# Gate and up projections of a two-layer encoder as seven block products, with the down projection as a phase of its own

## What is computed

```
mixed = jnp.concatenate([y_dil, y_na, y_conv], axis=-1) @ w_out
x = x + rmsnorm(mixed, g_post_mix)
hf = rmsnorm(x, g_pre_ffn)
f = (jax.nn.silu(hf @ w_gate) * (hf @ w_up)) @ w_down
return x + rmsnorm(f, g_post_ffn)
```

## Time and profile before

| | |
|---|---|
| time, median of 3 runs | 3253.07 us (3248.07 to 3254.09) |
| span of the profiled execution | 3252.3 us |
| busy: PE | 3189.5 us (98%) |
| busy: DVE, ACT, POOL | 46%, 29%, 28% |
| chain that ended last: PE, DVE, the engines' own issue | 88%, 7%, 2% |

### The profile page before, as it was taken

One profiled execution on the slowest core, in us unless ns is written; L12 is line 12 of the kernel. 1 busy time (PEld: TensorE's weight loads), 2 busy tenths in 40 slices (PEclk: granted clock), 3 DMA queues, 4 the chain that ended last, 5 costly groups with the idle time before them and its releaser, 6 DMA issues.

```text
span 3252.3 us, 42998 instructions
## 1 busy us (share of the span) xinstructions
PE 3189.5 (98%) x17580; PEld 2721.1 (84%) x17580; DVE 1507.1 (46%) x3072; ACT 937.1 (29%) x1816; POOL 903.9 (28%) x643
## 2 busy tenths in 40 slices
PE   9999999999999999999999999999999999999998
PEld 7888887888888888888878888878888888888887
DVE  6766657163333332333687666562533333333336
ACT  5433444441111111111344334444411111111112
POOL 1211113553222222221332121135622222222223
PEclk9999999999999999999999999999999999999999
DMA  3111002231111111110321110121311111110113
GB/s 146 45 54 51 23 34 81 79 130 52 39 40 39 34 38 39 40 39 33 128 83 49 51 48 29 42 82 70 124 54 38 39 39 39 39 39 33 39 40 123
DMA packets 50484, 184.29 MB, mean 57 GB/s; under 512 B 8049, under 2 KB 11761, under 8 KB 46833
## 3 DMA queue, kind: packets, MB, share of 16 engines
q1 hardware_dynamic: 47984, 173.68, 15.4%
q10 hardware_dynamic: 2304, 7.87, 0.6%
HBM read 144.81 MB, written 28.84 MB: 53 GB/s over the span
## 4 chain that ended last, share of the span: by engine, by line
PE 88%; DVE 7%; issue 2%; ACT 1%; DMA 1%; SPq 0%; POOL 0%; POOLq 0%; DVEq 0%; ACTq 0%
PE PS L1807 26%; PE PS L1809 26%; PE PS L1808 26%; PE PS L1959 3%; PE PS L1928 3%; PE PS L1943 2%; DVE PT L1557 1%; DVE XL L1390 1%; PE PS L1844 1%; DVE YO L1386 1%; DVE YO L1383 1%; DMA EYE<-small 0%; PE PS L1903 0%; ACT PT L1088 0%; DMA X<-mixed 0%
## 5 line engine op out<-in xcount | busy, mean ns | idle before, releaser
L1807 PE MATMUL PS<-XH,WH 128*128 128x512 f32 (+1 forms) x3648 | 1324.5, 363 | 19.8 <-DVE XL L1390 6.1
L1809 PE MATMUL PS<-XH,WL 128*128 128x512 f32 (+1 forms) x3648 | 1298.0, 356 | 0.0
L1808 PE MATMUL PS<-XL,WH 128*128 128x512 f32 (+1 forms) x3648 | 1297.1, 356 | 0.0
L1807 PEld LDWEIGHTS PS<-XH,WH 128*128 128x128 f32 x3648 | 691.3, 190 | 144.6 <-issue 25.2
L1809 PEld LDWEIGHTS PS<-XH,WL 128*128 128x128 f32 x3648 | 691.3, 190 | 100.9
L1808 PEld LDWEIGHTS PS<-XL,WH 128*128 128x128 f32 x3648 | 692.1, 190 | 92.2
L812 POOL TENSOR_TENSOR WL<-RAW,WH 128x1024 fp32r<-128x1024 f32 x188 | 448.7, 2406 | 361.1 <-ACT WH L984 361.1
L835 POOL TENSOR_TENSOR SG<-SG,RS 128x512 f32<-128x512 f32 x132 | 147.6, 1118 | 992.9 <-ACT SG L1127 992.9
L1627 DVE TENSOR_TENSOR ACC<-ACC,PS 128x512 f32<-128x512 f32 (+1 forms) x480 | 286.2, 598 | 245.3 <-PE PS L1809 244.0
L1807 PE MATMUL PS<-HH,WH 128*128 128x512 f32 (+1 forms) x1056 | 377.2, 357 | 3.6 <-DVE ACC L1627 2.0
L1809 PE MATMUL PS<-HH,WL 128*128 128x512 f32 (+1 forms) x1056 | 376.8, 357 | 0.0
(11 more groups left out here) (128 smaller groups left out, 3017.8 us busy)
## 6 DMA issues: line engine op xcount, KB each, us to landing
RAW<-w_in SPq DMA_DIRECT2D x48, 512.0 KB, 3.6
RAW<-w_gate SPq DMA_DIRECT2D x44, 512.0 KB, 3.4
RAW<-w_up SPq DMA_DIRECT2D x44, 512.0 KB, 3.5
RAW<-w_down SPq DMA_DIRECT2D x44, 512.0 KB, 3.7
X<-parked SPq DMA_DIRECT2D x6, 2048.0 KB, 7.3
RAW<-w_out SPq DMA_DIRECT2D x16, 512.0 KB, 4.0
parked<-YO SPq DMA_DIRECT2D x4, 2048.0 KB, 6.6
mixed<-YB ACTq DMA_DIRECT2D x8, 640.0 KB, 2.9
```

The source lines that it names most:

```text
L1807: nc.tensor.matmul(out, wh, xh, start=first, stop=False)
L1808: nc.tensor.matmul(out, wh, xl, start=False, stop=False)
L1809: return nc.tensor.matmul(out, wl, xh, start=False, stop=last)
```

## The change

Gate and up are written as one 2 x 2 block product. The model dimension is cut in two halves (4 tiles each) and so are the tokens of a group; gate and up of one unit are the two block rows of the weights; the seven products of the Strassen-Winograd scheme take the place of the eight block products. Their weight blocks are `A11`, `A12`, `A22` as loaded and four sums `S1` to `S4`; their token operands are `B11`, `B21`, `B22` and four sums `T1` to `T4`. Each product is 4 tiles x 3 matmuls into one PSUM bank.

- The tokens fall into group 0 (tokens 0 to 767, halves of 384) and group 1 (768 to 1279, halves of 256). A turn is one unit and one group: seven products, 84 matmuls, in three banks a, b, c. There are 44 turns in 27 visits: five visits of group 0 alone, 17 of both, five of group 1 alone. A visit loads its weights (1 MB), and DVE, ACT and POOL make the sums and the high and low parts of all seven blocks one visit ahead.
- The norm is applied to the tokens before the product (`normed`), so the two multiplications by `RS` behind it fall away. The recombination (`partial`: u2, u3, gate2, gate1, up2, hid1) is on DVE, with the copy of the first product on ACT (`first_copy`) and the second half's multiplication on POOL (`hidden2`).
- The hidden units go to memory (`store_hidden`) and come back (`load_hidden`) for the down product, now a phase after all gate and up turns: nine stages of two units and a last one of four, over six PSUM banks.
- The output projection and the norms around it go by four chunks (384, 384, 256, 256). In the passage to layer 1 the projections start only after the last down group, and POOL in place of DVE makes the low parts of chunks 0 and 1.

The core of the diff:

```
+OCHUNKS = ((0, 384), (384, 384), (768, 256), (1024, 256))
-STAGES = FT // 2
-END = STAGES - 1
+AHEAD = 5
+VISITS = [(u, (0,)) for u in range(AHEAD)] + [(u, (0, 1)) for u in range(AHEAD, FT)] + \
+         [(u, (1,)) for u in range(AHEAD)]
+TURNS = [(v, u, g) for v, (u, gs) in enumerate(VISITS) for g in gs]
+PRODUCTS = ("A11", "S2", "A12", "S3", "S1", "A22", "S4")
+OPERAND = {"A11": "B11", "A12": "B21", "A22": "T4", "S4": "B22", "S1": "T1", "S3": "T3", "S2": "T2"}
+END = 9
...
+            def turn_products(L, t):
...
+                for name in PRODUCTS:
+                    m, where = BLOCK[name], {"A11": "a", "A12": "a", "S1": "c", "S4": "c"}.get(name, "b")
...
+                    if name == "A12":
+                        pe.wait_ge(s_first, TURN[L, t])
+                    elif name == "S3":
+                        pe.wait_ge(s_u2, TURN[L, t])
+                    elif name == "A22":
+                        pe.wait_ge(s_u3, TURN[L, t])
+                    elif name == "S4":
+                        pe.wait_ge(s_gate2, TURN[L, t])
...
+                    for kk in range(4):
+                        last = products(PS[:, bank(t, where), 0:n], GH[v % 2][:, m, kk, :], GL[v % 2][:, m, kk, :],
+                                        CH[g][of][:, kk, :], CL[g][of][:, kk, :],
+                                        where not in opened and kk == 0, kk == 3, True)
```

What POOL runs, turn by turn (`TURNS`), in the changed kernel (`low` are low parts: `combination_low` of a token operand, 128 x 1024 in group 1, `raw_low` and `weight_sum_low` of a weight block, 128 x 512):

```
+                for t, (v, _, g) in enumerate(TURNS):
+                    first = t == 0 or TURNS[t - 1][0] != v
+                    if t in (2, 3):
+                        for k in range(KT):
+                            add(e, "x", t, k)
+                    if t == 5:
+                        for name in POOL_LOW[1]:
+                            combination_low(L, 1, name)
+                    if first and v + 1 < NV:
+                        raw_low(L, v + 1, 0)
+                        raw_low(L, v + 1, 1)
+                        if t in (2, 3):
+                            invert(e, "x", t)
+                        if t == 5:
+                            hidden2(L, t)
+                        weight_sum_low(L, v + 1, "S3")
+                        raw_low(L, v + 1, 2)
+                        weight_sum_low(L, v + 1, "S4")
+                    if t != 5:
+                        hidden2(L, t)
```

More of the change, by code:

```diff
@@ L526, in build @@
         s_yo = sem("yo")
-        s_gate = sem("gate")
-        s_sig = sem("sig")
-        s_sgr = sem("sgr")
-        s_h = sem("h")
+        s_pair = [sem(f"pair{i}") for i in range(2)]
+        s_wsum = sem("wsum")
+        s_whi = sem("whi")
+        s_wlo_raw = sem("wlo_raw")
+        s_wlo_v = sem("wlo_v")
+        s_wlo_p = sem("wlo_p")
+        s_xn = sem("xn")
+        s_mixsum = sem("mixsum")
+        s_chi = sem("chi")
+        s_clo_v = sem("clo_v")
+        s_clo_p = sem("clo_p")
+        s_product = sem("product")
+        s_first = sem("first")
+        s_u2 = sem("u2")
+        s_u3 = sem("u3")
+        s_gate2 = sem("gate2")
+        s_gate1 = sem("gate1")
+        s_silu2 = sem("silu2")
+        s_silu1 = sem("silu1")
+        s_up2 = sem("up2")
+        s_hid1 = sem("hid1")
+        s_hid2 = sem("hid2")
+        s_hout = [sem(f"hout{i}") for i in range(2)]
+        s_hin = [[sem(f"hin{i}{t}") for t in range(2)] for i in range(3)]
         s_hh = sem("hh")
@@ L666, in taps, with load_hidden @@
+            def load_hidden(L, part, t):
+                f = PARTS[part][2][t]
+                for turn in turns_of(f):
+                    sp.wait_ge(s_hout[turn % 2], stored(L, turn))
+                sp.dma_start(HF[HOME[part]][t][:, :], hidden[f, :, :]).then_inc(s_hin[HOME[part]][t], 16)
             def taps(L, j):
@@ L773, in _ @@
[L773 to L780 removed]
+                residual_mixed(e, 0)
+                store_mixed(e, 0)
+                residual_mixed(e, 1)
+                load_pair(L, 0)
+                store_mixed(e, 1)
@@ L781, in _ @@
+                for part in range(1, len(PARTS)):
+                    load_weights(L, part)
+                    load_hidden(L, part, 0)
+                    load_hidden(L, part, 1)
+                    if part == END and L + 1 < DEPTH:
+                        for unit in "kqv":
+                            load((L + 1, unit, 0))
                 e = 2 * L + 1
-                residual(e, 0)
-                residual(e, 1)
+                for c in range(NCH):
+                    residual(e, c)
@@ L953, in _ @@
+                for part in range(1, len(PARTS)):
+                    for f in PARTS[part][2]:
+                        low((L, "d", f))
+                e = 2 * L + 1
+                more_layers = L + 1 < DEPTH
+                for part in "kqv" if more_layers else ():
+                    low((L + 1, part, 0))
                 for k in range(KT):
@@ L974, in _ @@
                 else:
-                    scaled_gate(L, f + 1, 2)
+                    for k in range(KT):
+                        add(e, "y", 1, k)
+                    invert(e, "y", 1)
                     invert(e, "y", 2)
@@ L1743, in _ @@
+                for s in range(END):
                     for c in range(NCH):
@@ L1836, in sum_squares @@
                     pe.wait_ge(s_sq, SQUARE[e, kind, c, KT - 1])
-                    squares += [SQ[kind][:, m, :] for m in range(2)]
+                    squares += [pair_of(e, kind, c)[:, m, :] for m in range(2)]
                 else:
```

1370 lines of the change are left out of this document (777 added, 593 removed).

## The result

The changed kernel takes 3221.78 us (median of 4 runs, 3214.52 to 3224.54) against 3251.04 us for the kernel before beside it: a ratio of 0.9907, 95% interval 0.9893 to 0.9921. The gain is 29 us where 45 were forecast.

What follows compares the result with a forecast made beforehand. PE, busy 98% of the span, was taken as the bound; matmuls -119.6, output projection +5, waits +70, passage -3 and end +2.5 sum to -45 from 3252.3, forecasting 3208 us, range 3158 to 3243.

Steps and rivals of the forecast that it cites:

- main case: Whole kernel: the forecast sum with stalls of 45 to 95 us, giving 3183 to 3233 us; chance 0.60.
- matmul term: Gate and up: 1848 matmuls of each width replace 609.4 us per layer by 549.6, -119.6 us for both layers.
- Rival D: Gate and up: narrower matmuls cost more than the line says, 55 us for both layers, 3263 us; no separate chance.
- the clock: Gate and up: waits of several us lower PE's clock, costing 2.5 us more per layer.
- the hand-over from the output projection: Start of gate and up: PE waits for operands and their low parts, 5.5 us per layer (3 to 10).
- turns 1 to 6: Early gate and up: DVE and POOL need 97.8 us against PE's 77.9, so PE waits 20 us per layer.
- the visits of group 1 alone: Late gate and up: 11.3 us of work against 10.3, plus two down-weight low parts: 6 us per layer (0 to 12).
- Rival A: Gate and up: waits mostly absorbed, 12 us per layer, giving -91 us and 3162; chance 0.24 for 3145 to 3183.
- Rival B: Mixed visits: blocked DVE operations make each of 68 turns lose 1.3 us, 88 us in all, 3296; no separate chance.
- Rival C: Turns 1 to 6: waits chain up with low clock, 50 to 55 us per layer, 3235 to 3247; chance 0.07.
- The end: Last down stage and tail of the kernel: 53.3 us in place of 50.8, +2.5 us (0 to +7).
- The passage: Passage to layer 1: 24 us of waits and low clock in place of 26.9, -3 us (-8 to +8).

Runs made afterwards that it cites:

- no_lows: Changed kernel without POOL's five low parts of turn 5, PE taking the high part twice in group 1 instead: 3202.88 us.
- lows_dve: Changed kernel with the five low parts of group 1's operands made by DVE in place of POOL: 3209.47 us.
- late_steps: Changed kernel with DVE's steps 5 to 7 of chunks 2 and 3 put behind the next turn's u2: 3214.17 us.
- best: Changed kernel, eight visits of group 0 alone, group 1's low parts on DVE, operand work and norm steps spread over turns, end reordered: 3180.16 us, ratio 0.9785.
- double_early: Changed kernel with POOL making each weight low part twice in visits 7 to 21, the hidden product ahead of three low parts: 3219.88 us.

## Why the prediction was right, and where it was off

**The forecast's direction and mechanism held.** 3221.8 lies in 3158 to 3243 and in the main case's 3183 to 3233. Work of DVE and POOL that excludes each other makes PE wait on turns 0 to 6. For turns 5 and 6 no_lows and lows_dve show it. For turns 2 and 3 it is argued, from late_steps (the wait moved from u2 to u3) and from best (the same steps over more turns, and less waiting); no run takes POOL's work away there. That the total came within 14 us is in part luck: the matmuls gave 16 us more than forecast, and the rest cost 29 us more.

**The matmul term was too small by 16 us.** "96 of 256 take the rest" was the step that failed in it. The 192 wide matmuls of a stage do not all cost 0.2273: a down stage of 27.98 us less 48 narrow ones at 0.120 leaves 0.2315 for each of its 96 wide ones, and the fourth unit's 48 in the next gate and up stage take 11.15 us (1150.68 to 1161.83), 0.2323 each. I had given that rest to the narrow ones. These cost 0.1184 in the turns (9.94 / 84). The midpoint taken for 384, 0.1749, measures 0.1748 (14.68 / 84), so nearly the whole error is 1848 x 0.0041 = 7.6 us per layer. Rival D is refuted with it.

**Beside the matmuls the phases cost 95 us, not 70, and the term that was mis-sized is the clock.** PE's idle time was forecast at 32.5 us per layer and measures 28.5. By places: the hand-over from the output projection 5.5 and 3.7, turns 1 to 6 20 and 20.4, the visits of group 1 alone 6 and 2.7, the hand-over to the down phase 1 and 1.7 (for the low part of the last hidden value). The hand-over came out shorter although group 0's operands are 128 x 1536 and not the 1024 that my sum used (the low part for which PE waited 3.1 us took 3.4 us on POOL, DVE's next to it 4.8). The near match of turns 1 to 6 is in part luck. The sum took each DVE operation of 512 at 0.55 us where it takes 0.68 alone, but it counted the hidden product of turn 5 twice (1.0 us). And it put the wait at turns 5 and 6, where 9.7 us of it fell; 10.7 fell on turns 2 to 4, nearly all for u2 behind the norms' steps: PE's slack within a turn does not let a wait be caught up.

What the forecast lacked is 18.5 us of busy time per layer (19.6 in layer 1) beyond the turns' matmuls. Some 10 of them are matmuls at the lower clock, by the estimate above, where the forecast had 2.5; some 4 are the norms' 34 small matmuls, which now stand inside turns and which I had not counted. The rest, some 5 us, was not split; the first matmul behind each of the three long waits takes 0.55 to 0.66 us in place of 0.28 to 0.34, which the lower clock there explains in part. The forecast's own row had a larger price for the clock: a window of 86.10 us with 9.4 us of idle PE at 0.92 has lost up to 0.08 x 86.10 = 6.9 us, and I took 2.5 for 32.5 us of idle.

Visits of group 1 alone cost 4.6 us in all, and not by the mechanism that I gave: of PE's waits there (ACT `S1T` 1.3, DVE `U3T` 0.9, POOL `GL` 0.4) the smallest is for a low part of POOL. The largest, 1.14 us at 1260.78, stands behind ACT's high parts for the down phase (`WH` 1.05 and `HH` 1.25 us, from 1258.17 to 1260.28), which I had not counted on ACT at all.

Beside POOL's low parts DVE's 0.68 became 2.39 us, and POOL's 2.41 became 3.0 (mean of six, 128 x 1024); the DVE operation of 2.40 us ended at 809.59, 0.55 us after POOL's at 809.04. DVE's operations that read PSUM and one SBUF tile stayed at 0.55. The Trainium skill, page "SBUF — State Buffer", section "Who interferes with whom", says that a DVE instruction with at most one SBUF input stays clear of GpSimd and that one with two contends with it, an engine being held off for the whole of the other's instruction. The trace agrees on each of these three, with the 0.55, the 2.39 and the end at 809.59.

**Rival A** (waits mostly absorbed, 3162) was off by 60 us; its argument, DVE's idle half, counts an average where the work comes in a lump. **Rival B** did not occur; double_early shows that mixed visits bear 1.7 times POOL's work. **Rival C** named the low clock and was right in that alone: 47 us per layer, under its 50, but with less idle time than the main sum had. Its own times (3235 to 3247) are 1 to 3 us lower than its terms add up to.

**The end was +7, not +2.5**: the tail of 21 us was 22.8, and the last down stage cost 7.2 us more than its 28.0 in place of 4.3, by the norm's sums inside it (4.5 us) and 36 matmuls at 0.197 us behind them (the window 3186.90 to 3193.70 has a granted clock of 0.50). **The passage** was 4 us dearer than forecast: PE waited 6.6 us for `XL` and 4.2 for `RI`, both from POOL, about the 11 reckoned, the rest was dearer, at clock 0.92 as before. Neither was split further. **What stays open:** why wide matmuls space at either 0.227 or 0.232 us, the some 5 us per layer of busy time that were not split, and the 3 us that start and attention gained.

## What to carry to other kernels

An algorithm that takes matmuls away from PE pays in DVE and POOL work; add up, stage by stage and not over the span, the DVE operations with two SBUF inputs and all of POOL's as one resource, and look where this sum exceeds PE's time. There, moving five low parts from POOL to the "busier" DVE won 2.9 and 4.6 us per layer, and spreading the lump over more turns more than that. Price a wait of PE by the granted clock too: here 28.5 us of waits cost some 10 us more in matmuls at the lower level. And ask of every in-order list what stands behind the new work: POOL's late hidden product reached PE through a store and a copy two turns later.

## What the hardware showed that I had not expected

- The spacing of 512-column matmuls has two levels with the same code: in the changed kernel's down phase 96 of them take 22.3 to 22.4 us in some stages (0.2323 to 0.2333) and 21.8 in others (0.2271). Over the runs the down phase of a layer lasts 311.5 to 316.2 us. No run here tells why.
- POOL's operations grow too beside DVE's: the five low parts of 128 x 1024 in turn 5 take 2.8 to 3.35 us in place of 2.41, 0.4 to 0.9 more.
- The granted clock was 0.50 for 6.8 to 13.7 us from inside each of three waits of PE of 4.2 to 5.6 us.
- In double_early, with POOL busy 60% of the mixed visits (230.7 of 384.1 us) and DVE 45%, PE was never held up.
